# Order of GpSimd's weight sums in the down sets, and order of the opening's operand work, in a fused two-layer encoder step

## The reference

```python
def swiglu(x, w_gate, w_up, w_down):
    return (jax.nn.silu(x @ w_gate) * (x @ w_up)) @ w_down

for l in range(2):
    if l == 1:
        kv, b_logf = shared keys, values and forget gates from rms_norm(x, g_kv_b)
    x = x + 0.5 * swiglu(rms_norm(x, g_norm[l, 0]), w_ffn_gate[l, 0], w_ffn_up[l, 0], w_ffn_down[l, 0])
    h = rms_norm(x, g_norm[l, 1])
    x = x + attention(h) @ w_o        # layer 0: differential attention, layer 1: forgetting attention
    x = x + 0.5 * swiglu(rms_norm(x, g_norm[l, 2]), w_ffn_gate[l, 1], w_ffn_up[l, 1], w_ffn_down[l, 1])
y = rms_norm(x, g_final)
```

## Time and profile before

| | |
|---|---|
| median of 3 runs | 2457.02 us |
| lowest, highest | 2455.48, 2464.59 us |
| profiled execution | 2457.78 us, span 2455.7 us |
| PE busy | 2402.1 us, 98% |
| DVE busy | 1858.7 us, 76% |
| ACT busy | 1336.1 us, 54% |
| POOL busy | 544.4 us, 22% |
| DMA queues | loads by SP take 32.2% of the 16 engines' time, GpSimd's sums 21.9% |

### The profile page before, as it was taken

One profiled execution on the slowest core, in us unless ns is written; L12 is line 12 of the kernel. 1 busy time (PEld: TensorE's weight loads), 2 busy tenths in 40 slices (PEclk: granted clock), 3 DMA queues, 4 the chain that ended last, 5 costly groups with the idle time before them and its releaser, 6 DMA issues. The chain is left out here.

```text
span 2455.7 us, 48881 instructions
## 1 busy us (share of the span) xinstructions
PE 2402.1 (98%) x18377; PEld 2261.9 (92%) x18377; DVE 1858.7 (76%) x3709; ACT 1336.1 (54%) x2873; POOL 544.4 (22%) x422
## 2 busy tenths in 40 slices
PE   9899999999999999999999999999999999999998
PEld 9899999888778999999988999999996699999998
DVE  7887979422787888787925889787928878887865
ACT  6555656201785655555622655555618856555554
POOL 1222222354000121222135222222131002222210
PEclk9999999999999999999999999999999999999999
DMA  5557575333863465756523775766467544766642
GB/s 146 121 116 144 106 148 101 95 116 97 304 237 94 97 140 103 144 115 140 104 79 127 187 143 115 139 127 126 107 227 265 209 112 94 145 125 126 139 101 82
DMA packets 423237, 334.20 MB, mean 136 GB/s; under 512 B 20641, under 2 KB 383834, under 8 KB 423010
## 3 DMA queue, kind: packets, MB, share of 16 engines
q1 hardware_dynamic: 281296, 246.98, 32.2%
q0 software_dynamic: 133136, 65.82, 21.9%
q10 hardware_dynamic: 8578, 18.37, 2.1%
HBM read 314.98 MB, written 16.13 MB: 135 GB/s over the span
## 5 line engine op out<-in xcount | busy, mean ns | idle before, releaser
L997 PE MATMUL PS<-x_area,w_area 128*128 128x320 f32 x3096 | 483.1, 310 | 2.3 <-ACT PS L1804 2.3
L997 PEld LDWEIGHTS PS<-x_area,w_area 128*128 128x128 f32 x3096 | 461.6, 188 | 2.7 <-ACT PS L1804 2.6
L1718 ACT ACTIVATE w_area<-R 128x512 fp32r<-128x512 f32 (+2 forms) x583 | 325.5, 567 | 204.9 <-DVE R L2414 92.3
L2393 DVE TENSOR_TENSOR w_area<-R,w_area 128x512 fp32r<-128x512 f32 (+2 forms) x583 | 357.7, 615 | 87.1 <-ACT w_area L1718 86.5
L2393 DVE TENSOR_TENSOR r_area<-R,r_area 128x512 fp32r<-128x512 f32 (+2 forms) x437 | 265.8, 617 | 94.4 <-ACT r_area L1718 88.8
L1804 ACT ACTIVATE PS<-PS 128x320 f32<-128x320 f32 x438 | 178.3, 416 | 215.6 <-PE PS L997 189.9
L997 PE MATMUL PS<-r_area,w_area 128*128 128x320 f32 x1584 | 266.4, 311 | 10.7 <-ACT PS L1804 6.2
L1718 ACT ACTIVATE r_area<-R 128x512 fp32r<-128x512 f32 (+2 forms) x437 | 247.7, 567 | 47.2 <-DVE R L2414 20.2
L997 PEld LDWEIGHTS PS<-r_area,w_area 128*128 128x128 f32 x1584 | 239.1, 188 | 18.3 <-ACT PS L1804 11.2
L1226 PE MATMUL PS<-w_area,xn_hi 128*128 128x512 f32 x800 | 251.5, 396 | 0.5 <-DVE xT L2578 0.3
L997 PE MATMUL PS<-r_area 128*128 128x320 f32 x1392 | 236.5, 311 | 2.2 <-DVE r_area L2648 1.8
(11 more groups left out here) (348 smaller groups left out, 4152.6 us busy)
## 6 DMA issues: line engine op xcount, KB each, us to landing
R<-in_w_ffn_up_dram SPq DMA_DIRECT2D x45, 512.0 KB, 5.2
R<-in_w_ffn_gate_dram SPq DMA_DIRECT2D x43, 512.0 KB, 5.1
R<-in_w_ffn_up_dram SPq DMA_DIRECT2D x86, 256.0 KB, 4.1
R<-in_w_ffn_up_dram POOLq DMA_DIRECT2D x86, 256.0 KB, 4.8
R<-in_w_ffn_gate_dram SPq DMA_DIRECT2D x82, 256.0 KB, 4.6
R<-in_w_ffn_gate_dram POOLq DMA_DIRECT2D x81, 256.0 KB, 5.5
R<-in_w_ffn_down_dram SPq DMA_DIRECT2D x52, 384.0 KB, 3.9
R<-in_w_ffn_down_dram SPq DMA_DIRECT2D x88, 192.0 KB, 3.7
```

Source lines behind the costliest of these rows:

```text
L997: last = pe.matmul(PS[:, bank, 0:HT], a[:, k, :], b, start=(start and opens), stop=(k == n - 1 and a is lo), skip_group_check=True)
L1718: act.activation(role_parts(f, g, s, role)[0], role_source(f, g, s, role), ACT.Copy).then_inc(sem("early_cast") if key in EARLY_COUNT else ...
L2393: dve.tensor_tensor(lo, role_source(f, g, s, role), hi.bitcast(F32), ALU.subtract).then_inc(sem("early_split") if key in EARLY_COUNT else ...
```

## The change

Three things are moved; no computation is added or taken away.

GpSimd, in `add_sums`: for every down set the third sum goes out ahead of the first sum that stood before it in the queue. Where it was third(n), first(n+2) it is, around down sets, third(n+1), first(n+2). At the start of a group's down sets one third sum is thus pulled forward, and at its end two first sums stand together. The rows show GpSimd's DMAs from the last gate and up sets of the second group (f = 0) to its last down set, with what each waits for. Before:

```diff
--- before.py
+++ after.py
@@ -272,10 +272,11 @@
 
     plain = (by_block("5", "764"), by_block("15", "y26734"), by_block("15", "62734")[:-5] + [(x, 3) for x in "26734"])
     blocks = [("x", k) for k in range(KB)]
-    near = [("5", k) for k in range(4)]
+    near, far = ([(x, k) for k in range(4)] for x in "5y")
     opening = (by_operand("5764"),
-               blocks[:6] + near[0:1] + blocks[6:7] + near[1:2] + blocks[7:] + near[2:3] + by_operand("y") + near[3:] + by_operand("674"),
-               blocks[:6] + near[0:1] + blocks[6:7] + near[1:2] + blocks[7:] + near[2:] + by_operand("674"))
+               blocks[:2] + near[0:1] + blocks[2:3] + near[1:2] + blocks[3:6] + near[2:3] + far[0:1] + blocks[6:7] + near[3:] + far[1:2] + blocks[7:]
+               + far[2:] + by_operand("674"),
+               blocks[:2] + near[0:1] + blocks[2:3] + near[1:2] + blocks[3:6] + near[2:3] + blocks[6:7] + near[3:] + blocks[7:] + by_operand("674"))
     late = (by_operand("5764"), by_operand("5y764123"), by_operand("5761243"))
     return [opening, plain, late, plain]
 
@@ -875,8 +876,12 @@
                 order = chain(f)
                 for at in order[:2]:
                     first_sum(at)
+                ahead = [at for at in order[1:] if is_down(*at)]
                 for n, at in enumerate(order):
-                    third_sum(at)
+                    if at not in ahead:
+                        third_sum(at)
+                    if n + 1 < len(order) and order[n + 1] in ahead:
+                        third_sum(order[n + 1])
                     if n + 2 < len(order):
                         first_sum(order[n + 2])
 
@@ -1857,9 +1862,11 @@
                     for part in ("5", "7") if half == 0 else ("2", "4"):
                         hidden_rows(f, g, s, part)
 
-            def opening_down(f, prev, cur, then):
+            def opening_down(f, prev, cur, then, left=None):
 
                 copy_rows(f, *prev, 3)
+                if left is not None:
+                    left()
                 hidden_rows(f, *prev, "1")
                 copy_rows(f, *cur, 1)
                 role_high(f, *then, "W11")
@@ -1881,7 +1888,7 @@
                 for n, cur in enumerate(order):
                     prev, then = order[n - 1] if n else None, order[n + 1] if n + 1 < len(order) else None
                     if opens_down(*cur):
-                        opening_down(f, prev, cur, then)
+                        opening_down(f, prev, cur, then, after_set[1] if (f, n) == (0, 2) else None)
                         continue
                     if n >= 2:
                         copy_rows(f, *prev, 3)
@@ -1896,6 +1903,9 @@
                         copy_rows(f, *cur, 2)
                         copy_fifth(f, *cur)
                     role_high(f, *cur, "S4")
+                    if n == 1 and f == 0:
+                        copy_rows(f, *cur, 2)
+                        copy_fifth(f, *cur)
                     if n:
                         rows_on(f, *prev, 0)
                         if not third_first(f, cur):
@@ -1904,7 +1914,7 @@
                         role_high(f, *then, "W11")
                     if unsquared:
                         square(event, unsquared.pop())
-                    if n == 1:
+                    if n == 1 and f > 0:
                         copy_rows(f, *cur, 2)
                         copy_fifth(f, *cur)
                     if then is not None:
@@ -1925,7 +1935,7 @@
                         if n == 0:
                             copy_rows(f, *cur, 3)
                             copy_rows(f, *then, 1)
-                    if after_set is not None and n in after_set:
+                    if after_set is not None and n in after_set and (f, n) != (0, 1):
                         after_set[n]()
                     if finish_one is not None and cur[0] == len(GROUPS) - 1 and is_down(*cur):
                         tiles = 2 * (cur[1] - width(cur[0]) - 1)
@@ -2182,8 +2192,10 @@
                 act.wait_ge(sem("x_evac_dve"), k + 1)
                 act.wait_ge(sem("g_read"), 1)
                 x_high(0, 0, "x", k)
+                if k in (1, 2, 5, 6):
+                    x_high(0, 0, "5", k - 1 if k < 3 else k - 3)
                 if k >= 5:
-                    x_high(0, 0, "5", k - 5)
+                    x_high(0, 0, "y", k - 5)
                 if k == 0:
                     role_high(0, 0, 0, "W11")
                     role_high(0, 0, 0, "W21")
@@ -2218,14 +2230,14 @@
                 for k in range(4):
                     x_high(0, 0, x, k)
 
-            x_highs("y")
+            x_high(0, 0, "y", 3)
             role_high(0, 0, 1, "W21")
             role_high(0, 0, 1, "W22")
-            x_high(0, 0, "5", 3)
+            first_roles(0, 0, ("W11",))
             root(PS[:, 6:8, 0:HT])
             first_silu(0)
             first_silu(1)
-            first_roles(0, 0, ("W11", "S1"))
+            first_roles(0, 0, ("S1",))
             x_highs("6")
             first_roles(0, 0, ("S2",))
             first_hidden_cast("1")
@@ -3117,10 +3129,12 @@
                 dve.tensor_copy(xT[:, k, NP:T], PS[:, 7, 0:P]).then_inc(sem("x_evac_dve"), 1)
                 dve.wait_ge(sem("x_evac_dve"), k + 1)
                 dve.wait_ge(sem("x_evac_act"), k + 1)
-                if k >= 5:
-                    x_sum(0, 0, "5", k - 5)
+                if k in (1, 2, 4, 5):
+                    x_sum(0, 0, "5", k - 1 if k < 3 else k - 2)
+                if k in (2, 3, 6, 7):
+                    x_low(0, 0, "5", k - 2 if k < 4 else k - 4)
                 if k >= 6:
-                    x_low(0, 0, "5", k - 6)
+                    x_sum(0, 0, "7", k - 6)
                 block_low(k)
                 if k == 0:
                     role_low(0, 0, 0, "W11")
@@ -3146,7 +3160,7 @@
                 for k in range(4):
                     x_low(0, 0, x, k)
 
-            x_sum(0, 0, "5", 3)
+            x_sum(0, 0, "7", 2)
             dve.wait_ge(sem("x_squared"), ACT_SQUARES)
             dve.wait_ge(sem("x_squared_dve"), TB - ACT_SQUARES)
             eyes = ident.rearrange("p (o j) -> p o j", o=1).to_broadcast([P, TB, P])
@@ -3169,21 +3183,19 @@
                 marked(("gate", n), dve.scalar_tensor_tensor(out=tt[:, n, :], in0=tt[:, n, :], scalar=0.5, in1=rB[:, :], op0=ALU.mult,
                                                              op1=ALU.mult))
 
-            x_sums("7")
+            x_sum(0, 0, "7", 3)
+            x_sums("6")
             role_low(0, 0, 1, "W21")
-            role_low(0, 0, 1, "W22")
             first_gate(0)
             first_gate(1)
-            x_sums("6")
-            for k in range(2, 4):
-                x_low(0, 0, "5", k)
+            role_low(0, 0, 1, "W22")
+            x_sums("4")
             role_low(0, 0, 2, "W11")
             role_sum(0, 0, 2, "S2")
             role_low(0, 0, 2, "S1")
             first_scaled(0)
             first_scaled(1)
             first_hidden(0)
-            x_sums("4")
             role_low(0, 0, 2, "S2")
             x_lows("6")
             first_hidden(1)
```

## The result

| | before | after |
|---|---|---|
| median | 2457.51 us (4 runs) | 2518.01 us (4 runs) |
| lowest, highest | 2455.48, 2464.59 us | 2512.93, 2522.27 us |
| profiled span | 2455.7 us | 2510.8 us |
| PE busy | 2402.1 us | 2420.9 us |
| PE idle, summed over its timeline | 48.8 us | 85.1 us |

The ratio is 1.024, 95% interval 1.0212 to 1.0268. The kernel is slower by 60 us. I had forecast the right sign and, for the eleven second down sets of groups 2 to 4, the right place, but +14.6 us, and the time lies outside the range of 2450 to 2487 us.

What follows compares the result with a forecast made beforehand. TensorE, busy 98% of the span, was taken as the bound, leaving about 50 us to win. Opening -2.0, eleven places +12.1 and first groups +4.5 gave +14.6 us: 2471.6 us median, range 2450 to 2487.

Steps and rivals of the forecast that it cites:

- Part 1: Operands between the input blocks, 10 to 29 us: inserted DVE and ACT operations fit into waits, cost 0, at most +2 us.
- Parts 1 and 2: Opening, with two ACT copies moved up at 66 and 72 us: PE gains DVE's lead, -2.0 us, bounds 0 to 3.98.
- Part 3: GpSimd's order in down sets: first sum behind third lands at 195.05, +1.1 us at each of eleven places; first groups +4.5.
- my own sign, PE waiting 2 us and more: At each group's second down set: a PE wait this long would show that pairs of sums take what they take now.
- The bound "in time", 3.2 and 4.5 us: Second down set: first sums alone take 3.2 us least, 4.5 median, so landing at 193.0 to 194.3 costs 0 to 0.4.
- From the landing to PE: Second down set: no slack, so what delays DVE's sum of 193.95 delays PE by as much, +1.1 us.
- The first groups, +4.5 us: First group of each half, four times: smaller 128 KB sums land late by +1.1 us each; another meeting of sums taken as 0.
- +12.1 for the eleven places: Second down sets of groups 2 to 4 in four halves: 11 x 1.1 us of PE waiting for the late first sum.
- The rival of the pairs: Down sets: adjacent first and third sums land as late as existing pairs, +20 to +29 us, say 2484 us; chance 0.17.
- 11 x 2.6: Eleven second down sets: upper end of the loss if pairs take what they take now, giving +29 us.

## Why the prediction was wrong, point by point

- **Part 1, blocks at no cost.** Right. DVE's first operations inserted left its waits of about 1.1 us at about 0.4, and the blocks end within 0.1 us of where they did.
- **Parts 1 and 2, -2.0 us.** Right in mechanism and nearly in size. DVE's hidden low part, at 74.39 before, comes at

```profile
72.34 0.48 DVE L2660 SCALAR_TENSOR_TENSOR r_area<-tt,r_area 128x320 fp32r<-128x320 f32 x1
```

which is 2.05 us earlier, by DVE's lead. The two gaps on copies are gone, and one of 2.05 us on DVE's hidden low part stands in their place. PE reaches the same products ahead of the second down set 2.48 us earlier, at 83.91 (after) where it was at 86.39 (before). Only 0.9 us of it is idle time, with new gaps of 1.23 and 0.61 us on the same low part behind the first; 1.6 us is that the clock stayed at 1.00 here, which it did not before. The forecast had no such term, so that the size came out has some luck in it: in the run without GpSimd's order, which gave 3.4 us with bounds of 0.7 and 5.9, the half clock at this place was there again (0.66 from 73 to 77 us).
- **Part 3, "a cost of 195.05 - 193.95 = +1.1 us".** This is the step that failed. The place and the chain (third sum, first sum, DVE's sum, low part, PE) were as described. The landing was taken by bytes over a rate, as if the second sum could flow as soon as the engines were free. It landed 7.32 us after the third's issue in the median, not 6.5, 1.9 us late instead of 1.1. The rate itself held for the bulk: 95% of the two sums' bytes had moved 6.0 us after the third's issue, and what I had left out are the last packets, which came when the engines were nearly idle. That nothing else was in its way was wrong too: the loads of SyncE that had run beside the third sum alone now ran beside both, with a share of 1.01 from 196 to 198. The pairs of the earlier trace rows had shown 7.21 and 8.49 us for the same size, both inside the measured 6.86 to 8.59, and I set them aside on the ground of the loads beside them. They were the nearest rows. By my own sign, PE waiting 2 us and more, their rival is the one that holds.
- **The bound "in time", 3.2 and 4.5 us.** The earlier trace rows mixes sizes. The 3.2 us is of a sum of 128 KB; the 44 first sums of 192 KB took 3.67 us at the least and 3.9 in the median. So first(8) would have been just in time, had it gone as it did alone, and the 3.2 us that the prediction held against its estimate of 2.45 us is not of that size either; 3.67 us is still further from it. That the second sum makes the third land later shows only as 0.1 us (4.67 against 4.58 us in the median).
- **From the landing to PE.** I let PE wait as long as the sum is late. The gap grew by 2.2 us a place (28.1 against 3.5 us over eleven), not 1.1.
- **The first groups, +4.5 us.** I had one place in each; the traces show waits at the second down set, at the next one or at the next group's opening, 12.4 us more idle time over the four. The run with the new order in the third and fourth down set shows that the group's end is one of them, where first sums of the next group stand behind the last third sum. I had looked only for the second down set. And PE did not run through everywhere else, as I had read: at the first half's second down set the trace of before has a wait for ACT's copy, which stood behind a cast that waited for a sum. It says that ACT's queue is as close to PE as DVE's:

```profile
89.83 1.14 PE L997 MATMUL PS<-r_area,w_area 128*128 128x320 f32 x6 [1.52 <-ACT PS L1804]
```

- **The clock, missing altogether.** The forecast priced a wait at its length. PE's busy time grew by 18.8 us. Behind 14 of the long gaps in the down sets it ran at half clock for some 3 us, which cost 21.8 us, 1.5 us each as a rule. The opening's 1.6 us come off, and 1.7 us more, because the trace of before has half clock in an attention part (0.50 from 1955 to 1958 us) and the trace after has not; nothing in the change accounts for that. The trace of before had it to see, behind the gap of 2.29 us; its granted clock, the third figure from the end, was 0.63 over four us:

```profile
73.00:77.00 4.00, 4.00 (x18) 4.00 (x19) 3.81 (x9) 0.29 (x1) 0.00 (x0) 0.63 0.26 32
```

  Filling the waits with spare products shows that it is the standing still which costs it. The Trainium skill, TensorE: Matmul & The Clock Gate, "Part 1: The HAM clock gate", says that activity is what releases the slower state; the clock of 0.50 behind the gap and of 1.00 behind the filled one agree.
- **Sum.** Predicted +12.1 for the eleven places, measured 24.6 us idle; predicted +4.5, measured 12.4; predicted nothing, measured 21.8 of clock in the down sets; predicted -2.0, measured -2.5. With -1.7 of the attention part that is 54.6 of the span's 55.1 us. The rival of the pairs had the right landing, and was too low for the same missing term. Of its sum, "11 x 2.6" has no row: the second pair gives 3.1.

## What to carry to other kernels

A wait is queued in front of everything behind it on its engine, and here one late sum stood in the queues of two engines at once: moving the needed work ahead of the wait, on both, took 48 of 60 us away without touching the DMA order (some 7 us of these the moves give with the old order as well). Take the time of a DMA that follows another at once from pairs of its size in the trace, not from a rate: the rate told here when 95% of the bytes were there, and the rest came more than a microsecond later. And price a wait of TensorE with the slow clock behind it: here most waits of 2 us and more cost some 1.5 us on top.

## What was not expected of the hardware

In all fourteen traces, the one of before included, I counted PE's gaps ahead of the products of the half feed-forwards. Behind 82 of the 110 gaps of 1.9 us or more the granted clock fell to 0.50 within the next few microseconds, and behind 7 of the 98 gaps of 0.7 to 1.9 us. An accumulating DMA of 192 KB, issued 0.77 us behind another, landed 6.55 us after its own issue in the median, where the same ones alone took 3.8 us. The lateness is in the last bytes as well as in the shared engines: at the place shown the last 16 KB took 2 us, and for the last 2 us the DMA share was 0.12.
